# A transformer layer on eight cores: mixer laid out by channels, transposes moved to DMA, and the order of all engines taken from a planner

## The reference, cut to what matters

```python
proj = einsum('bsd,dc->bsc', x, w_in)                    # 1024 -> 512 (xp) | 512 (u) | 512 (v)
zg = gelu(proj[..., 512:])
# group A: 4 channel groups of 128, trailing mean over 2/4/8/16 tokens minus the token
pooled = (cs[t+1] - cs[t+1-w]) / min(t+1, w) - xp[t]     # cs: running sum over the tokens
pool_out = einsum('bsgc,gcd->bsgd', pooled, pool_w) * pool_scale
# group B: u * (W_s v + b), v layer-normed, W_s lower triangular 128x128 in chunks of 128 tokens
sgu_out = u * (einsum('hts,bnshd->bnthd', tril(w_s), layer_norm(v)) + b_s)
mix = einsum('bsc,cd->bsd', concat(pool_out, sgu_out), w_out)
h = layer_norm(alpha * x + mix)
y = layer_norm(alpha * h + (silu(h @ w_gate) * (h @ w_up)) @ w_down)   # 1024 -> 2 x 2816 -> 1024
```

## Time and profile before

| what | value |
|---|---|
| median of 3 runs | 2851.03 us (2850.96 to 2852.37) |
| profiled execution, its own time: span of the slowest core (core 4) | 2851.5 us |
| spans of the 8 cores | 2845.8 to 2851.5 us |
| PE busy | 2584.2 us, 91% of the span |
| DVE / ACT / POOL busy | 52% / 33% / 2% |
| mean granted PE clock, each core | 0.978 to 0.979 |
| DMA | 373.41 MB, 131 GB/s |

### The profile page before, as it was taken

The page is one execution under the profiler, slowest core; times in us unless marked ns, Lnnn a source line. Parts: engine busy times, 40 slices in busy tenths (PEclk is TensorE's granted clock), DMA queues, the critical chain, the costliest instruction groups (busy, mean ns, idle before and its releaser), DMA issues.

```text
span 2851.5 us, 37398 instructions; the slowest of 8 cores (2845.8 to 2851.5 us)
## 1 busy us (share of the span) xinstructions
PE 2584.2 (91%) x13300; PEld 1212.3 (43%) x13300; DVE 1488.5 (52%) x2500; ACT 943.8 (33%) x1300; POOL 50.3 (2%) x67
## 2 busy tenths in 40 slices
PE   3588999999999999999999999999999999999996
PEld 1243444444444444444444444444444444444442
DVE  1543554656455554654656555455644656455454
ACT  1232232433324234242433324233332423323220
POOL 2210000000000000000000000000000000000000
PEclk9799999999999999999999999999999999999998
DMA  9999443344434333443343434333443434344244
GB/s 181 130 166 163 135 147 111 118 129 131 133 120 138 115 122 127 140 133 111 126 130 122 141 126 133 109 121 130 143 136 111 138 109 140 129 130 144 88 144 138
DMA packets 153830, 373.41 MB, mean 131 GB/s; under 512 B 57776, under 2 KB 64304, under 8 KB 153648
## 3 DMA queue, kind: packets, MB, share of 16 engines
q1 hardware_dynamic: 98880, 347.91, 38.6%
q0 software_dynamic: 54768, 23.11, 8.0%
HBM read 360.52 MB, written 50.86 MB: 144 GB/s over the span
## 4 chain that ended last, share of the span: by engine, by line
PE 77%; DVE 7%; DMA 6%; ACT 5%; issue 4%; another core or an unknown queue 0%; DVEq 0%; POOL 0%; ACTq 0%; SPq 0%; POOLq 0%
PE ps L582 19%; PE ps L710 18%; PE ps L585 18%; PE ps L380 11%; PE ps L500 7%; DMA sb_wgur<-scr_gu 2%; DMA scr_gu<-w_gate_up 2%; ACT L594 2%; PE ps L272 2%; DMA sb_poolw<-pool_w 1%; DVE sb_silr L596 1%; DVE sb_hr L257 1%; ACT sb_silr L594 1%; ACT L246 1%; DVE sb_sgr L475 1%
## 5 line engine op out<-in xcount | busy, mean ns | idle before, releaser
L582 PE MATMUL ps<-sb_hT,sb_wgur 128*128 128x512 bf16 x2816 | 676.7, 384 | 21.1 <-DMA sb_wgur<-scr_gu 21.1
L585 PE MATMUL ps<-sb_hT,sb_wgur 128*128 128x512 bf16 x2816 | 669.3, 381 | 0.0
L710 PE MATMUL ps<-sb_wdnr,sb_aT 128*128 128x512 bf16 x2816 | 638.6, 379 | 10.5 <-PE ps L710 1.8
L596 DVE SCALAR_TENSOR_TENSOR sb_silr<-sb_silr,ps 128x512 f32<-128x512 f32 x352 | 240.1, 682 | 482.0 <-ACT sb_silr L594 481.5
L585 PEld LDWEIGHTS ps<-sb_hT,sb_wgur 128*128 128x128 bf16 x2816 | 277.2, 98 | 337.8 <-issue 10.1
L582 PEld LDWEIGHTS ps<-sb_hT,sb_wgur 128*128 128x128 bf16 x2816 | 273.1, 99 | 342.2 <-issue 34.2
L710 PEld LDWEIGHTS ps<-sb_wdnr,sb_aT 128*128 128x128 bf16 x2816 | 267.8, 98 | 345.0 <-issue 43.3
L380 PE MATMUL ps<-sb_win,sb_xTr 128*128 128x512 bf16 x1536 | 357.8, 391 | 60.3 <-DVE sb_xTr L280 58.0
L594 ACT ACTIVATE sb_silr<-ps 128x512 f32<-128x512 f32 x352 | 210.1, 597 | 433.5 <-PE ps L585 405.7
L594 ACT ACT_TABLE_LOAD x150 | 192.4, 1283 | 447.0 <-PE ps L585 445.6
L599 DVE SCALAR_TENSOR_TENSOR sb_aT<-sb_silr,ps 128x512 bf16<-128x512 f32 x352 | 242.2, 688 | 64.0 <-DVE sb_silr L596 62.4
(11 more groups left out here) (55 smaller groups left out, 1351.1 us busy)
## 6 DMA issues: line engine op xcount, KB each, us to landing
sb_wgur<-scr_gu SPq DMA_DIRECT2D x352, 512.0 KB, 4.0
sb_wdnr<-scr_dn SPq DMA_DIRECT2D x160, 512.0 KB, 4.4
sb_xr<-x SPq DMA_DIRECT2D x64, 512.0 KB, 3.9
out<-sb_hr SPq DMA_DIRECT2D x64, 512.0 KB, 5.7
scr_gu<-w_gate_up POOLq DMA_DIRECT2D x44, 256.0 KB, 26.6
sb_wdnr<-scr_dn SPq DMA_DIRECT2D x32, 256.0 KB, 4.1
scr_dn<-w_down POOLq DMA_DIRECT2D x10, 512.0 KB, 48.9
sb_win<-w_in POOLq DMA_DIRECT2D x1, 3072.0 KB, 34.8
```

What stands on the lines that cost most here:

```text
L582: ins = t.matmul(ps[:, bg, :], lhsT=wgur[:, s, k, 0:128], rhs=hT[:, k, :], start=(k == 0), stop=(k == 7))
L585: ins = t.matmul(ps[:, bu, :], lhsT=wgur[:, s, k, 128:256], rhs=hT[:, k, :], start=(k == 0), stop=(k == 7))
L596: S.task("dve", lambda v: v.scalar_tensor_tensor(out=silr[:, q, :], in0=silr[:, q, :], scalar=1.0, in1=ps[:, bg, :], op0=ALU.add, op1=ALU. ...
L710: ins = t.matmul(ps[:, bd[b], :], lhsT=aT[:, k, b * 128:(b + 1) * 128], rhs=wdnr[:, s, kk, :], start=(k == 0), stop=(k == NJ - 1))
```

## The change

The kernel is written anew around the same FFN.

- **Layout.** The host also hands over x transposed, by tiles (`xT`), and POOL's queue loads it as bf16 (`load_xT`). The mixer works on 512 tokens at once: V (v with tokens on the partitions, 4 x 8 matmuls), U and P (u and the pooling input with channels on the partitions, each 4 x 8 matmuls), S (gating, 16 matmuls of 128 columns), O (output projection, 8 x 8 matmuls).
- **Pooling** is a running sum on DVE (`tensor_tensor_scan`, L509) and one more pass (L513). `pool_w` and `pool_scale` are multiplied into the first half of `w_out` once, at the start.
- **h is transposed by DMA** from ACT's queue (`dma_start_transpose`), through two bf16 buffers `hb`.
- **Layer norm:** 1/sqrt is two POOL instructions (L438, and L441 with the operation pow) in place of ACT's square root and DVE's reciprocal.
- **FFN weights** are loaded as f32 to bf16 straight into SBUF for tile 0 (a ring `wr` of six slots), and SP writes each chunk back to DRAM for the other tiles.
- **Order.** Every instruction or DMA is a task with a duration and a position (`pos`); `Plan.schedule` picks the task that can start first, then the lowest position, and also gives out the PSUM banks. Its costs are fixed numbers in the file (a matmul group 8 x 216 ns, a DMA 2 us and 250 bytes per ns). The engines then run the planned order, again with semaphores.

The core of the diff, cut:

```diff
-        def flush_sqrt():
-            for r in pending_sqrt:
-                S.task("act", lambda a, r=r: a.activation(out=lnst[:, r, 14:15], in_=lnst[:, r, 13:14],
-                                                          func=AF.Sqrt, bias=EPS, scale=1.0),
-                       reads=[f"lnmv{r}"], writes=[f"lnsd{r}"])
-            pending_sqrt.clear()
...
-        def tr_pe(src_ap_fn, n, src_names, c):
-            b = bank()
-            c["trb"] = b
-            pv = ps[:, b, :].bitcast(BF16)
-
-            def f_tr(t):
-                for k in range(n):
-                    ins = t.transpose(pv[:, k * 128:(k + 1) * 128], src_ap_fn(k), ident[:])
-                return ins
-            S.task("pe", f_tr, reads=list(src_names) + ["ident"], excl=[bn(b)])
...
-        def conv_gu(j):
-            S.dma("pool", scr_gu[j, :, :, 0:128], w_gu_v[:, :, j * 128:(j + 1) * 128], writes=[f"scrgu{j}a"])
-            S.dma("pool", scr_gu[j, :, :, 128:256], w_gu_v[:, :, DFF + j * 128:DFF + (j + 1) * 128],
-                  writes=[f"scrgu{j}b"])
...
-        def P7(gb):
-            hb, pos = gb % HB, gb % 4
-            c = {}
-            return (lambda: tr_pe(lambda k: hbr[:, hb, k * 128:(k + 1) * 128], 8, [f"hb{hb}"], c),
-                    lambda: tr_evac(8, hT[:, :, pos * 128:(pos + 1) * 128], [f"hT{pos}"], c))
...
+class Plan:
+
+    SEM = 90.0
+    DMA_FIX = 2000.0
+    DMA_RATE = 250.0
...
+            t0, e, usable = best
+            now = [(t.pos, t.seq, t) for r, t in usable if r <= t0 + 1e-9]
+            t = min(now, key=lambda q: q[:2])[2]
...
+            t.start = t0
+            if t.kb is None:
+                free[e] = t0 + t.dur
+                t.end = free[e]
+            else:
+                free[e] = t0 + t.dur
+                dma_free = max(dma_free, free[e]) + t.kb * 1024.0 / self.DMA_RATE
+                t.end = dma_free + self.DMA_FIX
...
+            for s in t.succ:
+                s.ready = max(s.ready, t.end + (self.SEM if s.eng != e or t.kb is not None else 20.0))
+                s.npred -= 1
+                if s.npred == 0:
+                    cand[s.eng].append(s)
...
+        order.sort(key=lambda t: (t.start, t.seq))
...
+        def dma(q, out, in_, kb, pos, reads=(), writes=(), transpose=False):
+            def fn(e):
+                if transpose:
+                    return e.dma_start_transpose(out=out, in_=in_)
+                return e.dma_start(out=out, in_=in_)
+            return P.add(q, fn, 1000.0 if q == "pool" else 60.0, pos, reads, writes, kb=kb)
...
+        def load_xT(mt, pos):
+            for k in range(0, 8, 4):
+                dma("pool", xT[:, k:k + 4, :], xT_d[mt][:, k:k + 4, :], 1024, pos, writes=[f"xT{k}"])
...
+        def ln_rstd(r, b0, b1, pos):
+            nm = [f"mv{r}{b}" for b in range(b0, b1)]
+            rs = [f"rs{r}{b}" for b in range(b0, b1)]
+            P.add("pool", lambda e: e.tensor_scalar(out=rst[:, r, b0:b1], in0=mvt[:, r, b0:b1, 1], scalar1=EPS,
+                                                    scalar2=1.0, op0=ALU.add, op1=ALU.mult),
+                  300, pos, reads=nm, writes=rs)
+            P.add("pool", lambda e: e.tensor_tensor(out=rst[:, r, b0:b1], in0=rst[:, r, b0:b1],
+                                                    in1=nhalf[:, b0:b1], op=ALU.pow),
+                  600, pos, reads=["nhalf"] + rs, writes=rs)
...
+                        i = e.matmul(ps[:, bk.home, :], lhsT=wu[:, h, k, :], rhs=xT[:, k, :],
+                                     start=(k == 0), stop=(k == 7))
+                    return i
+                P.add("pe", pe, 8 * 216, q, reads=["xT0", "xT4", f"wu{h}"], banks=[bk], alloc=[bk])
+                P.add("act", lambda e, h=h, bk=bk: e.activation(out=guT[:, h, :], in_=ps[:, bk.home, :],
+                                                                func=AF.Gelu),
+                      c_act(512), q, writes=[f"gu{h}"], banks=[bk])
...
+                P.add("dve", lambda e, g=g, w=w, s2=s2: e.tensor_tensor_scan(
+                    out=sw[:, s2, :], data0=xp[:, g, 16:XP0 + 512], data1=xp[:, g, 16 - w:XP0 + 512 - w],
+                    initial=0.0, op0=ALU.add, op1=ALU.subtract),
+                    c_dve(528), q, reads=[f"xp{g}", f"xh{g}", "xz"], writes=[f"sw{s2}"])
+                P.add("dve", lambda e, g=g, w=w, s2=s2: e.scalar_tensor_tensor(
+                    out=mixT[:, g, :], in0=sw[:, s2, 16:528], scalar=1.0 / w, in1=xp[:, g, XP0:XP0 + 512],
+                    op0=ALU.mult, op1=ALU.subtract), c_dve(512), q,
+                    reads=[f"sw{s2}", f"xp{g}"], writes=[f"mix{g}"])
...
+            if mt + 1 < NMT:
+                load_xT(mt + 1, pos("P", 3))
...
+                    def pe(e, b=b, n=n, bk=bk):
+                        for k in range(8):
+                            i = e.matmul(ps[:, bk.home, :], lhsT=mixT[:, k, b * 128:(b + 1) * 128],
+                                         rhs=wout[:, k, n * 512:(n + 1) * 512], start=(k == 0), stop=(k == 7))
+                        return i
+                    P.add("pe", pe, 8 * 216, q, reads=[f"mix{k}" for k in range(8)] + [f"wo{k}" for k in range(8)],
...
+                ln_stats(r1, b, hr[:, hs, :], D, f"h{hs}", q)
+                ln_rstd(r1, b, b + 1, q)
+                ln_apply(r1, b, hr[:, hs, :], g1B[:], b1B[:], f"h{hs}", "g1B", "b1B", q)
+                P.add("act", lambda e, hs=hs, b=b: e.activation(out=hb[:, b % 2, :], in_=hr[:, hs, :], func=AF.Copy),
+                      c_act(1024), q, reads=[f"h{hs}"], writes=[f"hb{b % 2}"])
+                dma("act", hT[:, :, b * 128:(b + 1) * 128], hb[:, b % 2, :], 512, q,
+                    reads=[f"hb{b % 2}"], writes=[f"hT{b}"], transpose=True)
...
+        def fetch_gu(mt, j, pos):
+            s = wslot()
+            v = wr[:, s, :].rearrange("p (k c) -> p k c", k=8)
+            if mt == 0:
+                dma("pool", v, wgu_d[j], 1024, pos, writes=[f"w{s}"])
+                dma("sp", scr_gu[j], v, 512, pos + 2, reads=[f"w{s}"], writes=[f"sg{j}"])
+            else:
+                dma("sp", v, scr_gu[j], 512, pos, reads=[f"sg{j}"], writes=[f"w{s}"])
+            return s
...
+        offs = {"V": (0.5, 1.5, 2.5, 3.5), "U": (4.5, 5.5, 6.5, 7.5), "P": (8.5, 9.5, 10.5, 11.5),
+                "S": (13.5, 14.5, 15.5, 16.5), "O": (19.5, 21.5, 23.5, 25.5)}
...
+            base = 34.0 * mt
+            ffn_up(mt, base)
...
+                mixer(mt + 1, lambda st, i: base + offs[st][i])
+            ffn_down(mt, base)
```

1015 lines of the change are left out of this document (456 added, 559 removed).

## The result

The changed kernel takes 2512.25 us (median of five runs, 2508.5 to 2530.2) against 2852.37 of the kernel before on the same chip: a ratio of 0.882, 95% interval 0.879 to 0.885.

The account below looks back on a forecast made before the run. PE was taken as the bound, busy 91% of the span. First chunk 128 us, remaining work 2333, late chunks 15, waits 15 x 1.0 and tail 24.4 sum to 2516 us; range 2465 to 2560 (57%).

Parts of the forecast that it names:

- the bound of 0.6: Steady tile: the least PE waits expected, 0.6 us, from two down groups directly following another in the same banks.
- the slack: End of a tile: DVE frees banks after 28.3 us, PE wants them after 24 to 33, leaving 2 to 5 us.
- The second rival: Every tile: PE's waits stay at 13.4 us because the fixed order meets other durations than planned; 2702 us, 8%.
- the 193 us: Whole run: the part of the forecast gain that comes from PE's waits, beside 14 from the start and 129 from work.
- the 13.4 us a tile: Steady tile of the kernel before: time that is not PE work, 169.9 us less 156.5 of work.
- One sign of being wrong: Layer norm: DVE rows that idle behind POOL would show the prediction wrong; no size was given.
- The third rival: Layer norms at a tile's end: POOL late by two DVE passes, 8.3 us a tile lost; 2640 us, 14%.
- the 2.9 plus a few: Transposing DMA of h: a block takes 2.9 us plus a few to land, which is hidden.
- the fourth rival: Transposing DMAs of h land in 26.6 us one after another, PE waits 50 us a tile; 3260 us, 6%.
- late chunks: Tile 0: weight chunks that come late to a ring of six cost 15 us.
- PE's 174: First chunk to tile 0's last down group: 800 large matmuls on PE, 174 us, against 165 us of DMA.
- The first rival: Start and tile 0: f32 loads run at 184 GB/s, first chunk at 193 us; 2656 us, 15%.

Follow-up runs that it names:

- packed: The change with PE's order fixed by position and V, U, P, S, O of the next tile in one block behind chunk 21: 2724 us, ratio 0.955.
- spread fixed order: The change with PE's order fixed by the written positions, V, U, P, S, O standing one by one between gate/up chunks: 2576 us, ratio 0.903.
- the other start: The change with later pool_w fold, reordered loads, 16 POOL DMAs in flight, last tile by blocks and PE's order fixed by positions: 2552 us, ratio 0.894.

## Why the prediction held, point by point

**PE's work.** 149.4 us a tile was right: 149.38 measured. In the run with PE's transposes a steady tile grew by the 1.8 us of their work and by 0.8 to 1.1 more.

**The waits.** 1.0 us a tile was taken; from 460 to 2480 us PE waited for no other engine, under the bound of 0.6: O and V pieces stand between the down groups, and where they don't, groups of the two halves alternate, so that none of the twelve directly follows another in the same banks. The prediction had read two such places out of the order; there is none. The 11 us that remain lie in the tile behind tile 0, 6.5 of them in one wait. There DVE does three layer norms first (its timeline, and PE's):

```profile
302.90 2.48 DVE L654 SCALAR_TENSOR_TENSOR sb_hr<-sb_hr,ps 128x512 f32<-128x512 f32 x4 [17.85 <-PE ps L644]
...
318.80 0.68 DVE L625 SCALAR_TENSOR_TENSOR sb_sil<-sb_sil,ps 128x512 f32<-128x512 f32 x1
```

```profile
319.63 3.57 PE L463 MATMUL ps<-sb_wv,sb_xT 128*128 128x512 bf16 x8 [6.48 <-DVE sb_sil L625]
```

This is the tile-end stall that the slack was worked out for; in later tiles DVE's order takes L625 between the passes of the first layer norm (2231.41 us in the tile that starts at 2226.82). The second rival (waits stay) came true only where an experiment changed the order.

**The source of the 193 us.** That most of them go with the new order is borne out. The packed and the spread fixed order differ in positions alone, by 148 us, and in the kernel before the square root accounts for 2.8 of the 13.4 us a tile, about a fifth. That the old layout could not have had such an order is not shown: two orders of it gave nothing, both with a fault of their own. What the prediction didn't see is how much hangs on where the planner's order settles: edits of the start and the tail turned 2512 into 2898.

**1/sqrt on POOL.** A pair was put at 0.2 to 1.7 us, with 1.7 taken; its two instructions take 0.74 us alone and 1.15 in the mean, and one pair reaches 2.4. One sign of being wrong did show: DVE idles behind POOL for 85 us over the span. Yet from 460 to 2480 us none of that reaches PE, so the slack hides it. POOL's timeline, and DVE's beside the second power:

```profile
2225.92 0.55 POOL L441 TENSOR_TENSOR sb_rst<-sb_rst,sb_nhalf 128x1 f32<-128x1 f32 x1
...
2230.25 1.65 POOL L441 TENSOR_TENSOR sb_rst<-sb_rst,sb_nhalf 128x1 f32<-128x1 f32 x1
```

```profile
2230.22 1.27 DVE L446 SCALAR_TENSOR_TENSOR sb_hr<-sb_hr,sb_mvt,sb_g2B 128x1024 f32<-128x1024 f32 x1
```

The power that starts with DVE's pass takes 1.65 us, the other 0.55; of 192 powers, 69 that overlap such a pass for long take 1.33 to 1.67, and 120 take 0.55. The Trainium skill ("GPSIMD Engine Reference", section 1) says that POOL shares its SBUF interfaces with VectorE and meets contention where DVE has two SBUF inputs; the trace agrees. The third rival, one power late by two passes, did not come; and its price, 8.3 us a tile, was too high: with pairs that are 2.1 to 3.8 us later a steady tile costs some 2.2 us more.

**h by DMA.** A block lands in 4.4 us (median of 64; 3.1 to 34.3): the 2.9 plus a few taken. The 26.6 of the fourth rival is real too, but only beside the f32 loads of tile 0: one of the 64 on core 0, at 34.3 us, where the others take 6.7 at most; on core 5 of the fixed order and core 0 of the other start all four of tile 1 were about as late. The Trainium skill ("Advanced Engine Details and Errata", section "X-Bar Transpose (TRN2)") has transposing DMAs as fast as regular ones; the traces don't bear that out: in a steady tile a block of 256 KB takes 4.4 us, as long as the 3.2 to 4.1 us in which plain loads of twice the bytes land, and beside the f32 loads it takes far longer. As a term of the sum, 1.8 us of PE work a tile were saved without a wait in the steady part.

**The start.** 128 us predicted, 123.5 measured, with two steps off that partly cancel. The loads up to tile 1's x came at 97 us instead of 107; V, U, P and the half of S behind them took 26 us instead of 20.7, a wait of 3.0 among them. And the loads were not the only path: PE ran the mixer of tile 0 late, having waited 26.5 us for `pool_wT`, and its O ended at 99.2 us, where V of tile 1 began. The two paths ended within 2 us of each other. Where the wait for `pool_wT` was taken out (the two runs with another start), V of tile 1 waited some 20 us for `xT` instead, and the first chunk stayed at 124 and 125 us. The first 1/sqrt pair came at 54.8 us against 59.

From there to tile 0's last down group 179.3 us passed against 189: late chunks took 5 instead of 15. PE's 174 met 173.6 in part by luck, since 784 large matmuls were run there and not 800; the other 16 came later. The first rival, f32 loads at 184 GB/s, did not come.

**The tail.** 23.1 us against 24.4.

**The sum.** 128 + 189 + 2174 + 24.4 against 123.5 + 179.3 + 2181.5 + 23.1 us: errors of 1 to 10 us that partly cancel. That the total came within 4 us is luck to that extent; that it came within the stated range is not.

**ACT.** Eight table loads a tile were expected, from the kernel's mix of functions; there is one in the whole run (L414, 1.3 us). Before had 308, 304 of them at the square root and at the first function behind it. Nothing hung on it but ACT's share (16% instead of 33%).

## What to carry to other kernels

Count the work of the bound engine and its waits apart, and read the waits from where a step stands, not from how busy its producer is: here the same instructions took 2512, 2576, 2724 and, with small edits, 2898 us by their order alone. An unchanged total may hide two effects: POOL's pair in the kernel before made each steady tile 2.8 us shorter and tile 0 45 us longer, so look at the start and at a steady tile apart. Before a small step goes to another engine, look at what stands in front of it there: here it was DMA issues, and PE waited 56 us. After an edit anywhere in a planned program, look at the steady order again, since a planner may settle elsewhere.

## What was not expected of the hardware

- Transposing DMAs of 256 KB (rows of 256 bytes) beside f32 loads that convert and their write-backs: 27 to 43 us to landing on core 0 of one run and core 5 of another, against 3.1 at the least in a steady tile, and in one of them the rate of all DMA stays at 50 GB/s or less for most of 10 us.
- gelu, tanh and copy alternate on ACT for 2500 us with one table load; the square root brings back at least 278.
- A power on POOL takes 0.55 us alone and 1.33 to 1.67 where a DVE pass with two SBUF inputs covers it; passes with one input in PSUM leave it at 0.55.
- An instruction on POOL behind twelve DMA issues waits for each of them: put into the kernel before, the first 1/sqrt pair came so late that DVE stood still for 59.8 us.
- A scan of 528 elements on DVE takes 1.25 us, where other passes of 512 take 0.68.
- In the change PE's 6.5 us wait (313 to 320 us) is followed by a granted clock of 0.91 from 320 to 340 us, where PE does not stop, and 1.00 from 340 us on: part of that stretch ran at 1.2 instead of 2.4 GHz.
